# A streaming encoder step: the gate's third of the modulation summed on VectorE instead of TensorE

## The chip, the cores and the metric

The kernel runs on one core of one Trainium2 chip. The metric is the device time of one execution in microseconds (us). A core has TensorE (PE, matrix products), VectorE (DVE), ScalarE (ACT), GpSimd (POOL) and SyncE (SP, which here only issues DMAs), all running their own programs in order and waiting for each other by semaphores.

## What is computed

A one-layer encoder. Each row of x is normalised, scaled and shifted by terms that come from a conditioning vector c, and projected; attention and a pooling mixer run on the projections, and the result is gated by a third term from c. The part that matters here:

```python
def ada_terms(c, w_ada, b_ada):
    m = jax.nn.silu(c) @ w_ada + b_ada          # w_ada is 1024 x 3072
    shift, scale, gate = jnp.split(m, 3, axis=-1)
    return shift, scale, gate

def project(x, c, norm_g, w_ada, b_ada, w_in, b_f):
    shift, scale, gate = ada_terms(c, w_ada, b_ada)
    h = rmsnorm(x, norm_g) * (1.0 + scale[:, None, :]) + shift[:, None, :]
    p = h @ w_in
    ...

def merge(x, attn, ag, pool, pg, gate, w_out):
    z = jnp.concatenate([attn * jax.nn.silu(ag), pool * jax.nn.silu(pg)], axis=-1)
    return x + gate[:, None, :] * (z @ w_out)
```

There are 2048 prompt rows and 64 sample rows, with a c of their own each: two vectors of 1024. Shift and scale are needed before the first projection, the gate only in `merge`, the last stage.

## The kernel before, in words

The kernel has three stages, one behind the other: `stage_project`, attention and the output. The change lies in `stage_project`, which has three phases.

**Start.** SP issues the loads in the order of its program: the first two thirds of w_ada (`slab`), the weights of the value projection (`vraw`), and then the gate's third of w_ada (`graw`, four DMAs of 1 MB). TensorE forms shift and scale with `slab` and the two silu vectors (`pair`, two columns for each of the eight k tiles of 128 rows).

**Value phase.** A loop over 17 tiles of 128 rows. For each, TensorE turns rows (`turn`, into the PSUM pair `xps`), VectorE modulates (`modulate`), ScalarE and GpSimd split the result into a high and a low part (`hhi`, `hlo`), and TensorE multiplies (`value`, L552). Before the tile with `t == GATE_AT` (3) TensorE runs `gate()` (L537): 16 matmuls with a 2-column stationary and 512 moving columns, in fp32, into one slot of `xps`; VectorE adds the bias (L917) and SP stores the row to `scratch_gate`.

**Projection tiles.** 20 tiles of 128 output columns in the order K0, Q0, U0, PG0, and so on (numbered 0 to 19), each of five chunks of columns (three of 512, two of 288; `acc` is a ring of five PSUM banks). Every engine walks the one list `PROJECT_EVENTS` in order and does its own part of each entry. An entry ("weights", n+1) stands at the head of tile n: SP loads the weights of the next tile into `wraw`, ScalarE rounds them to `whi` (L706), GpSimd forms `wlo` (L514). For a chunk of K or Q ScalarE writes `ohi` (L780), VectorE `olo` (L959), the "split", and SP stores both. Entry "f_turn" at the end of tile 0 makes SP issue 22 small DMAs; "k_rows" stores a K chunk in another layout and comes one chunk later. `mps` is a ring of three PSUM banks for these side products. ScalarE writes the chunks of a U tile to `u`, from which VectorE makes the pooling sums.

These lines show how a list entry ties the engines together, on SP and on VectorE:

```python
            for kind, x in PROJECT_EVENTS:
                if kind == "weights":
                    load_weights(sp, x)
                elif kind == "chunk":
                    if x.i >= 1:
                        store_chunk(sp, TILE_CHUNKS[x.i - 1])
...
                if kind == "chunk" and x.tile.split:
                    use = HL_USES[x.i]
                    dve.wait_ge(split_hi, SPLIT_CHUNKS.index(x.i) + 1)
```

## Time and profile before

| | |
|---|---|
| three runs | 1428.19 us median (1426.74 to 1432.84) |
| the profiled execution | 1433.23 us, of which the span of the core 1431.5 us |
| TensorE busy | 1298.6 us (91%), 7007 matmul records |
| VectorE busy | 716.8 us (50%) |
| ScalarE busy | 569.9 us (40%) |
| GpSimd busy | 179.6 us (13%) |
| mean granted TensorE clock | 0.945 of full speed |

The profile is a record of one execution. Times in it are in us from the start of the span. A timeline line gives start, length, engine, source line, operation, output<-input, the count of merged instructions, and in brackets the idle time of the engine before it with what ended that. A line of stretches gives the length, then busy time and count for PE, PE's weight loads, DVE, ACT and POOL, then the granted clock and the DMA share. One fp32 matmul leaves two records.

### The profile page before, as it was taken

To read this page: it belongs to the slowest core of one execution; us is meant where nothing else is said; L and a number is where in the kernel's file an instruction comes from. 1 tells how busy PE (TensorE), PEld (TensorE's weight loads), DVE (VectorE), ACT (ScalarE), POOL (GpSimd) and SP (SyncE) were. 2 spreads that over 40 slices of the span, in tenths; PEclk is the share of its full clock that TensorE was granted. 3 is DMA by queue.
4 is the path that set the end of the run, shared out by engine and by line. 5 is a ranking of instruction groups with operands and counts; after the bars stand their busy time and mean duration, and the time that the engine had idled before them with its cause. 6 is when DMAs were issued, how large, how long until landed. Compare 5 with 4: busy or idle time off the path is not lost. (4 is left out here: it accounts for less than half of the span.)

```text
span 1431.5 us, 19348 instructions
## 1 busy us (share of the span) xinstructions
PE 1298.6 (91%) x7007; PEld 1049.6 (73%) x7007; DVE 716.8 (50%) x1973; ACT 569.9 (40%) x1158; POOL 179.6 (13%) x196
## 2 busy tenths in 40 slices
PE   7899999999999999995699989999999991599996
PEld 1779988888888888885576676767767671488884
DVE  1646433244461111000588877888788881334434
ACT  3546411212112121111477676776777670211111
POOL 1213301101001010100000230131032023000000
PEclk9899999999999999998599999999999995799998
DMA  9636344112213434223913655739456413756662
GB/s 365 232 118 195 141 140 127 60 46 76 87 46 126 155 123 142 88 68 97 199 21 57 105 96 122 136 70 173 82 100 105 94 31 104 251 162 192 206 191 88
DMA packets 159644, 179.51 MB, mean 125 GB/s; under 512 B 34073, under 2 KB 123533, under 8 KB 154878
## 3 DMA queue, kind: packets, MB, share of 16 engines
q1 hardware_dynamic: 153294, 155.21, 42.0%
q10 hardware_dynamic: 5824, 21.50, 4.5%
q8 instruction: 56, 0.92, 0.3%
q0 software_dynamic: 432, 1.57, 0.3%
q14 instruction: 38, 0.31, 0.1%
HBM read 111.55 MB, written 66.69 MB: 125 GB/s over the span
## 5 line engine op out<-in xcount | busy, mean ns | idle before, releaser
L597 PE MATMUL prj_acc<-prj_hhi,til_whi 128*128 128x512 f32 (+1 forms) x800 | 286.5, 358 | 0.0
L599 PE MATMUL prj_acc<-prj_hlo,til_whi 128*128 128x512 f32 (+1 forms) x800 | 284.1, 355 | 0.0
L598 PE MATMUL prj_acc<-prj_hhi,til_wlo 128*128 128x512 f32 (+1 forms) x800 | 284.1, 355 | 0.0
L1386 ACT ACTIVATE att_whi<-att_tps 128x512 fp32r<-128x512 f32 x336 | 169.2, 516 | 118.8 <-PE att_tps L1352 116.0
L1416 DVE TENSOR_TENSOR att_wlo<-att_tps,att_whi 128x512 fp32r<-128x512 f32 x336 | 189.9, 584 | 32.1 <-ACT att_whi L1386 31.8
L1406 DVE TENSOR_SCALAR_CACHE_REDUCE att_wx<-att_sps 128x512 f32<-128x512 f32 x192 | 113.4, 619 | 131.0 <-PE att_sps L1337 127.0
L1336 PE MATMUL att_sps<-att_ka,att_qa 128*128 128x512 f32 (+4 forms) x328 | 153.3, 467 | 25.6 <-DMA att_kb<-scratch_fkd 23.7
L599 PEld LDWEIGHTS prj_acc<-prj_hlo,til_whi 128*128 128x128 f32 x800 | 150.8, 189 | 21.4
L597 PEld LDWEIGHTS prj_acc<-prj_hhi,til_whi 128*128 128x128 f32 x800 | 150.8, 189 | 20.9
L598 PEld LDWEIGHTS prj_acc<-prj_hhi,til_wlo 128*128 128x128 f32 x800 | 150.9, 189 | 20.7
L1524 PE MATMUL fin_acc<-fin_whi,fin_zh 128*128 128x512 f32 (+1 forms) x272 | 106.8, 393 | 45.1 <-DMA fin_zl<-scratch_z 45.1
L1364 PE MATMUL att_ops<-att_whi,att_vt 128*128 128x512 f32 x336 | 140.2, 418 | 0.0
L1352 PE MATMUL att_tps<-keep_ident,att_wx 128*128 128x128 f32 x672 | 118.1, 297 | 12.1 <-ACT att_wx L1380 7.4
L1337 PE MATMUL att_sps<-att_kb,att_qb 68*128 68x512 f32 (+4 forms) x328 | 126.9, 387 | 0.0
L1364 PE MATMUL att_ops<-att_wlo,att_vt 128*128 128x512 f32 x336 | 124.3, 371 | 0.0
L1352 PEld LDWEIGHTS att_tps<-keep_ident,att_wx 128*128 128x128 f32 x672 | 84.5, 151 | 43.9 <-issue 23.4
L1380 ACT ACTIVATE att_wx<-att_wx,att_nm 128x1024 f32<-128x1024 f32 (+1 forms) x96 | 99.0, 1033 | 29.5 <-DVE att_nm L1411 29.5
L1525 PE MATMUL fin_acc<-fin_wlo,fin_zh 128*128 128x512 f32 (+1 forms) x272 | 106.6, 392 | 0.0
L1526 PE MATMUL fin_acc<-fin_whi,fin_zl 128*128 128x512 f32 (+1 forms) x272 | 106.4, 391 | 0.0
L959 DVE SCALAR_TENSOR_TENSOR til_olo<-prj_acc,til_ohi 128x512 fp32r<-128x512 f32 (+1 forms) x40 | 23.8, 597 | 155.0 <-ACT til_ohi L780 155.0
L1336 PEld LDWEIGHTS att_sps<-att_ka,att_qa 128*128 128x128 f32 (+1 forms) x328 | 67.5, 206 | 45.3 <-DMA att_kb<-scratch_fkd 23.9
L514 POOL TENSOR_TENSOR til_wlo<-til_wraw,til_whi 128x1024 fp32r<-128x1024 f32 x20 | 48.1, 2406 | 408.7 <-ACT til_whi L706 408.7
(182 smaller groups left out, 1915.5 us busy)
## 6 DMA issues: line engine op xcount, KB each, us to landing
til_wraw<-in_w_in SPq DMA_DIRECT2D x20, 512.0 KB, 4.2
att_ka<-scratch_k SPq DMA_DIRECT2D x16, 560.0 KB
scratch_v<-val_vs SPq DMA_DIRECT2D x17, 512.0 KB, 4.4
att_qa<-scratch_q SPq DMA_DIRECT2D x16, 528.0 KB
val_xt<-in_x_prompt ACTq DMA_DIRECT2D x16, 512.0 KB, 4.4
ini_al<-in_w_ada SPq DMA_DIRECT2D x8, 1024.0 KB, 15.7
fin_zh<-scratch_z SPq DMA_DIRECT2D x16, 512.0 KB, 4.4
fin_zl<-scratch_z SPq DMA_DIRECT2D x16, 512.0 KB, 5.8
```

What stands on the lines that cost most here:

```text
L597: pe.matmul(out, w[0][:, k, :], hhi[:, k, cs], start=(k == 0), stop=False)
L598: pe.matmul(out, w[1][:, k, :], hhi[:, k, cs], start=False, stop=False)
L599: mm = pe.matmul(out, w[0][:, k, :], hlo[:, k, cs], start=False, stop=(k == KT - 1))
L1336: pe.matmul(bank[0:x.m, 0:x.n], qa[e][:, q], ka[e][:, k], start=True, stop=False)
L1337: mm = pe.matmul(bank[0:x.m, 0:x.n], qb[e][:, q], kb[e][:, k], start=False, stop=not x.last)
L1352: mm = pe.transpose(bank[:, t * P:(t + 1) * P], weights(st, 4 * st.c + t)[:, x.w0:x.w0 + P], keep["ident"][:, :])
L1364: mm = pe.matmul(bank[:, x.skip:x.width], vt[e][0:x.keys, x.tile, :], part[b][0:x.keys, x.skip:x.width], start=(x.first and part is whi), ...
L1386: act.activation(whi[x.i % W_RING][0:x.keys, x.skip:x.width], tps[x.i % T_RING][0:x.keys, x.skip:x.width], ACT.Copy).then_inc(hi_ok, 1)
L1406: dve.tensor_scalar(weights(st, x.row)[0:x.m, x.w0:x.w0 + x.n], sps[x.i % S_RING][0:x.m, 0:x.n], 1.0, None, ALU.mult, ALU.max, accum_out=t ...
L1416: dve.tensor_tensor(wlo[b][0:x.keys, x.skip:x.width], tps[x.i % T_RING][0:x.keys, x.skip:x.width], raw(whi[b][0:x.keys, x.skip:x.width]), ...
L1524: pe.matmul(out, zh[b][:, k, 0:n], whi[:, k, cols], start=(k == 0), stop=False)
L1525: pe.matmul(out, zh[b][:, k, 0:n], wlo[:, k, cols], start=False, stop=False)
```

## The change

The gate's matmuls leave the value phase, and so do the load of the gate's third of w_ada, its bias, the addition and the store. In their place the list gets entries in the tiles 0 and 1:

- "gate_in" x (SP): load the k tile x of the gate's weights, 128 x 1024 fp32 (512 KB), into one of two slots of `gw`. From x = 2 on it waits until both sums of k tile x-2 are done.
- "gate" x (VectorE): for each of the two vectors one pass over 128 x 1024: `gs[w] = gw * pair` (x = 0, `tensor_scalar`) or `gs[w] += gw * pair` (x >= 1, `scalar_tensor_tensor`).
- "gate_bias" (SP): load of the bias into `gw`.
- "gate_sum" 0 and 1, behind the last chunk of tile 1: TensorE adds up the 128 partitions with the constant `pick`, two fp32 matmuls of 512 columns for each half; VectorE adds the bias; SP stores to `scratch_gate`.

`gw` and `gs` share memory with `u`, so the first chunk of tile 2 waits on ScalarE for the store of the gate. The waits on `g_ok` and `g_out` in the value phase go, and `turn` uses the two `xps` slots in plain alternation.

```diff
@@ project_events
+    gates = {(0, 3): [("gate_in", 0), ("gate_in", 1)], (0, 4): [("gate", 0), ("gate_in", 2)],
+             (1, 0): [("gate", 1), ("gate_in", 3), ("gate", 2), ("gate_in", 4)],
+             (1, 1): [("gate", 3), ("gate_in", 5), ("gate", 4), ("gate_in", 6)],
+             (1, 2): [("gate", 5), ("gate_in", 7), ("gate", 6)], (1, 3): [("gate", 7), ("gate_bias", 0)],
+             (1, 4): [("gate_sum", 0), ("gate_sum", 1)]}
...
+            ev += gates.get((t.n, c), [])
@@ SP
-            for k in range(0, KT, 2):
-                sp.dma_start(graw[:, k:k + 2, :], wada[:, k:k + 2, 2 * D:]).then_inc(g_in, 16)
-            sp.wait_ge(m_full, 1)
-            sp.dma_start(gate_b, io["b_ada"][:, 2 * D:].partition_broadcast(2)).then_inc(gb_in, 16)
...
-                if t == GATE_AT:
-                    sp.wait_ge(g_ok, 2)
-                    sp.dma_start(dram["gate"][:, :], grow).then_inc(g_out, 16)
...
+                elif kind == "gate_in":
+                    if x >= 2:
+                        sp.wait_ge(ga_ok, 2 * (x - 1))
+                    sp.dma_start(gw[:, x % 2, :], wada[:, x, 2 * D:]).then_inc(g_in[x % 2], 16)
+                elif kind == "gate_bias":
+                    sp.wait_ge(ga_ok, 2 * (KT - 1))
+                    sp.dma_start(gate_b, io["b_ada"][:, 2 * D:].partition_broadcast(2)).then_inc(gb_in, 16)
+                elif kind == "gate_sum" and x == 1:
+                    m_wait(sp, m_free, ("gate_sum", 1), 1)
+                    sp.dma_start(dram["gate"][:, :], grow).then_inc(g_out, 16)
@@ TensorE
-                if t == GATE_AT:
-                    gate()
...
+                elif kind == "gate_sum":
+                    pe.wait_ge(pick_ok, 3)
+                    pe.wait_ge(ga_ok, 2 * KT)
+                    for w in range(2):
+                        mm = pe.matmul(bank[0:2, :], pick[:, 2 * w:2 * w + 2], gs[:, w, x * 512:(x + 1) * 512],
+                                       start=(w == 0), stop=(w == 1))
+                    mm.then_inc(m_done, 1)
@@ ScalarE
-                if t == KT:
-                    act.wait_ge(g_out, 16)
...
+                        if x.c == 0 and t.g == 0:
+                            act.wait_ge(g_out, 16)
@@ VectorE
-                if t == GATE_AT:
-                    dve.wait_ge(g_full, 1)
-                    dve.wait_ge(gb_in, 16)
-                    for n in range(2):
-                        cs = slice(n * 512, (n + 1) * 512)
-                        dve.tensor_tensor(grow[:, cs], xps[GATE_SLOT][0:2, cs], gate_b[:, cs], ALU.add).then_inc(g_ok, 1)
...
+                elif kind == "gate":
+                    dve.wait_ge(g_in[x % 2], 16 * (x // 2 + 1))
+                    for w in range(2):
+                        if x == 0:
+                            ins = dve.tensor_scalar(gs[:, w, :], gw[:, 0, :], pair[:, 0, w:w + 1], None, ALU.mult)
+                        else:
+                            dve.wait_ge(ga_ok, 2 * x - 1 + w)
+                            ins = dve.scalar_tensor_tensor(out=gs[:, w, :], in0=gw[:, x % 2, :], scalar=pair[:, x, w:w + 1],
+                                                           in1=gs[:, w, :], op0=ALU.mult, op1=ALU.add)
+                        ins.then_inc(ga_ok, 1)
+                elif kind == "gate_sum":
+                    m_wait(dve, m_done, ("gate_sum", x), 1)
+                    dve.wait_ge(gb_in, 16)
+                    cs = slice(x * 512, (x + 1) * 512)
+                    dve.tensor_tensor(grow[:, cs], mps[M_USES["gate_sum", x].slot][0:2, :], gate_b[:, cs], ALU.add).then_inc(m_free, 1)
```

On VectorE the row of instructions from the first chunk of tile 1 on was, before:

```order
L959 SCALAR_TENSOR_TENSOR til_olo<-prj_acc,til_ohi 128x512 [waits prj_t_split_hi]
L992 COPY til_row<-prj_mps 128x128 [waits prj_row_out0,prj_t_m_done]
L992 COPY til_row<-prj_mps 96x128
L992 COPY til_row<-prj_mps 64x128
L959 SCALAR_TENSOR_TENSOR til_olo<-prj_acc,til_ohi 128x512 [waits prj_t_split_hi] x2
```

and is now, in the same place (`prj_g_in0` and `prj_g_in1` are the landings in the two slots of `gw`):

```order
L955 SCALAR_TENSOR_TENSOR til_olo<-prj_acc,til_ohi 128x512 [waits prj_t_split_hi]
L1003 COPY til_row<-prj_mps 128x128 [waits prj_row_out0,prj_t_m_done]
L1003 COPY til_row<-prj_mps 96x128
L1003 COPY til_row<-prj_mps 64x128
L986 SCALAR_TENSOR_TENSOR gat_gs<-gat_gw,prj_silu,gat_gs 128x1024 [waits prj_ga_ok,prj_g_in1]
L986 SCALAR_TENSOR_TENSOR gat_gs<-gat_gw,prj_silu,gat_gs 128x1024 [waits prj_ga_ok]
L986 SCALAR_TENSOR_TENSOR gat_gs<-gat_gw,prj_silu,gat_gs 128x1024 [waits prj_ga_ok,prj_g_in0]
L986 SCALAR_TENSOR_TENSOR gat_gs<-gat_gw,prj_silu,gat_gs 128x1024 [waits prj_ga_ok]
L955 SCALAR_TENSOR_TENSOR til_olo<-prj_acc,til_ohi 128x512 [waits prj_t_split_hi]
```

The sums of k tiles 1 and 2 stand behind the split of the first chunk and its k_rows copies; those of 3 and 4, 5 and 6, and 7 follow behind the splits of the next three chunks.

On SP the same stretch, before:

```order
L465 DMA out_k_prompt<-til_row 128x2x128 [waits prj_t_m_free]
L465 DMA out_k_prompt<-til_row 32x128
L377 DMA til_wraw<-in_w_in 128x8x128 [waits prj_t_wt_lo]
L386 DMA scratch_k<-til_ohi 128x288 [waits prj_t_free_d]
L387 DMA scratch_k<-til_olo 128x288
L465 DMA out_k_prompt<-til_row 128x128 [waits prj_t_m_free]
L465 DMA out_k_prompt<-til_row 96x128
L465 DMA out_k_sample<-til_row 64x128
L386 DMA scratch_q<-til_ohi 128x512 [waits prj_t_free_d]
L387 DMA scratch_q<-til_olo 128x512
```

and now:

```order
L459 DMA gat_gw<-in_w_ada 128x1024 [waits prj_ga_ok]
L380 DMA til_wraw<-in_w_in 128x8x128 [waits prj_t_wt_lo]
L389 DMA scratch_k<-til_ohi 128x288 [waits prj_t_free_d]
L390 DMA scratch_k<-til_olo 128x288
L471 DMA out_k_prompt<-til_row 128x128 [waits prj_t_m_free]
L471 DMA out_k_prompt<-til_row 96x128
L471 DMA out_k_sample<-til_row 64x128
L459 DMA gat_gw<-in_w_ada 128x1024 [waits prj_ga_ok] x2
L389 DMA scratch_q<-til_ohi 128x512 [waits prj_t_free_d]
L390 DMA scratch_q<-til_olo 128x512
L459 DMA gat_gw<-in_w_ada 128x1024 [waits prj_ga_ok] x2
```

The first of these rows is the load of k tile 2, ahead of the weights of tile 2; the two pairs are those of the k tiles 3 and 4, and 5 and 6, each waiting for sums of VectorE; the load of k tile 7 follows behind the next pair of Q stores. The two loads without a wait (k tiles 0 and 1) stand in tile 0, ahead of the 22 DMAs of "f_turn".

## Rows read from the trace of the kernel before

**Rows 1.** Stretches of the project stage; columns as told above, clock before DMA share.
```profile
49.00:71.00 22.00, 21.97 (x161) 21.54 (x162) 11.06 (x43) 11.47 (x21) 7.18 (x3) 0.88 0.50 163
71.00:85.30 14.30, 14.30 (x41) 3.41 (x39) 3.19 (x11) 4.00 (x7) 2.35 (x1) 1.00 0.31 99
85.30:176.00 90.70, 90.70 (x765) 90.45 (x763) 49.98 (x186) 49.75 (x91) 30.04 (x13) 1.00 0.51 161
176.00:250.00 74.00, 72.24 (x373) 61.64 (x373) 27.34 (x71) 15.29 (x30) 7.20 (x3) 0.98 0.45 133
```

**Rows 2.** Timeline of TensorE around the gate's matmuls.
```profile
70.61 13.89 PE L537 MATMUL vps_xps<-ini_ah,prj_silu 128*2 128x512 f32 x32
84.44 0.77 PE L529 MATMUL vps_xps<-keep_ident,val_xn 128*128 128x128 f32 x5
```

**Rows 3.** Timeline of TensorE, the turns of two successive tiles of the value phase.
```profile
91.13 1.04 PE L529 MATMUL vps_xps<-keep_ident,val_xn 128*128 128x128 f32 x8
...
97.77 1.04 PE L529 MATMUL vps_xps<-keep_ident,val_xn 128*128 128x128 f32 x8
```

**Rows 4.** Timeline of TensorE, the first matmul of tile 2.
```profile
229.85 0.39 PE L597 MATMUL prj_acc<-prj_hhi,til_whi 128*128 128x512 f32 x1
```

**Rows 5.** Timeline of SP: k_rows in tile 0, end of f_turn, weights of tile 2.
```profile
204.29 0.39 SPq L465 DMA_DIRECT2D out_k_prompt<-til_row  x1
...
216.35 0.30 SPq L459 DMA_DIRECT2D scratch_fkd<-fgt_fr  x1
...
217.65 0.42 SPq L377 DMA_DIRECT2D til_wraw<-in_w_in  x1
```

**Rows 6.** Timeline of ScalarE: weights of tile 2, then tile 1's first two chunks.
```profile
222.12 1.06 ACT L706 ACTIVATE til_whi<-til_wraw 128x1024 fp32r<-128x1024 f32 x1 [15.05 <-DMA til_wraw<-in_w_in]
223.09 1.07 ACT L780 ACTIVATE til_ohi<-prj_acc 128x512 fp32r<-128x512 f32 x2
```

**Rows 7.** Timeline of VectorE: end of tile 0, split of tile 1's first chunk, k_rows.
```profile
208.25 0.60 DVE L992 COPY til_row<-prj_mps 128x256 f32<-128x256 f32 x2
223.70 0.69 DVE L959 SCALAR_TENSOR_TENSOR til_olo<-prj_acc,til_ohi 128x512 fp32r<-128x512 f32 x1 [14.85 <-ACT til_ohi L780]
224.31 0.67 DVE L992 COPY til_row<-prj_mps 128x128 f32<-128x128 f32 x3
```

**Rows 8.** Line 1574, a scalar_tensor_tensor on VectorE: durations in ns min/median/max.
```profile
L1574 DVE SCALAR_TENSOR_TENSOR fin_o<-fin_y,fin_st,fin_fg x17: 1277/1285/1286, 1259.2 to 1426.8; 128x1024 f32<-128x1024 f32 x16, 64x1024 f32<-64x1024 f32 x1
```

**Rows 9.** Line 655, loads of x, 512 KB each: issue, and issue to landing.
```profile
L655 ACTq DMA_DIRECT2D val_xt<-in_x_prompt x16: 334/335/446, 0.8 to 133.4; - x16
...
DMA to landing us min/median/max: 3.6/4.4/8.6
```

**Rows 10.** Line 377, loads of projection weights, 512 KB each, likewise.
```profile
L377 SPq DMA_DIRECT2D til_wraw<-in_w_in x20: 380/433/1226, 166.7 to 616.5; - x20
...
DMA to landing us min/median/max: 3.9/4.2/5.3
```

**Rows 11.** Stretches behind idle time of TensorE: one in tile 0, two in attention.
```profile
184.00:190.00 6.00, 6.00 (x21) 4.83 (x21) 2.42 (x12) 2.52 (x4) 2.39 (x1) 0.72 0.17 50
...
690.00:695.00 5.00, 5.00 (x13) 3.60 (x13) 4.12 (x12) 1.36 (x3) 0.00 (x0) 0.50 1.17 208
...
705.00:710.00 5.00, 5.00 (x21) 3.88 (x20) 2.38 (x8) 2.03 (x5) 0.00 (x0) 0.53 1.00 211
```

**Rows 12.** Longest wait of TensorE in front of attention: us in total, times, longest.
```profile
PE att_sps L1336 <- DMA att_kb<-scratch_fkd: 23.7, 1, 23.7
```

**Rows 13.** Timeline, two VectorE operations of one shape, the second beside a GpSimd one.
```profile
273.98 0.69 DVE L1019 TENSOR_TENSOR til_olo<-til_row,til_ohi 128x512 fp32r<-128x512 f32 x1 [0.70 <-ACT til_ohi L797]
...
284.55 2.41 POOL L514 TENSOR_TENSOR til_wlo<-til_wraw,til_whi 128x1024 fp32r<-128x1024 f32 x1 [27.50 <-ACT til_whi L706]
...
286.11 1.39 DVE L1019 TENSOR_TENSOR til_olo<-til_row,til_ohi 128x512 fp32r<-128x512 f32 x1 [0.70 <-ACT til_ohi L797]
```

**Rows 14.** Timeline of ScalarE: weights of tile 3.
```profile
238.73 1.06 ACT L706 ACTIVATE til_whi<-til_wraw 128x1024 fp32r<-128x1024 f32 x1 [4.72 <-DMA til_wraw<-in_w_in]
```

More of the change, by code:

```diff
@@ L144, in chunk_in @@
     return lambda kind, x: kind == "chunk" and x.tile.kind in kinds
-M_USES = uses(lambda kind, x: kind in ("cache", "state", "f_sum", "f_turn", "k_rows", "mix", "tails"), M_RING)
+M_USES = uses(lambda kind, x: kind in ("cache", "state", "f_sum", "f_turn", "k_rows", "mix", "tails", "gate_sum"), M_RING)
 F_EV = {}
@@ L200, in stage_project @@
         tri = s.sb("tri", [P, P])
+        pick = s.sb("pick", [P, 4])
         with Scope(nc, "val") as a:
@@ L230, in stage_project @@
             gsc = b.sb("gsc", [P, T])
+            with Scope(nc, "gat") as g:
+                gw = g.sb("gw", [P, 2, D])
+                gs = g.sb("gs", [P, 2, D])
+            u = b.sb("u", [P, U_ALL])
+            dhi = [b.sb(f"dhi{n}", [P, 512], F32R) for n in range(D_RING)]
+            dlo = [b.sb(f"dlo{n}", [P, 512], F32R) for n in range(D_RING)]
             sa = b.sb("sa", [P, HIST + 512])
             sb_ = b.sb("sb", [P, HIST + 512])
-            dhi = [b.sb(f"dhi{n}", [P, 512], F32R) for n in range(D_RING)]
-            dlo = [b.sb(f"dlo{n}", [P, 512], F32R) for n in range(D_RING)]
         with Scope(nc, "vps") as a:
@@ L252, in stage_project @@
         x_in = [s.sem(f"x_in{n}") for n in range(2)]
+        g_in = [s.sem(f"g_in{n}") for n in range(2)]
         v_out = [s.sem(f"v_out{n}") for n in range(2)]
@@ L530, in turn @@
                 mm.then_inc(xturn, 1)
-            def gate():
-                pe.wait_ge(g_in, 64)
-                pe.wait_ge(hf_ok, KT * (GATE_AT + 1))
-                for n in range(2):
-                    for k in range(KT):
-                        mm = pe.matmul(xps[GATE_SLOT][0:2, n * 512:(n + 1) * 512], pair[:, k, :], graw[:, k, n * 512:(n + 1) * 512],
-                                       start=(k == 0), stop=(k == KT - 1))
-                mm.then_inc(g_full, 1)
             def value(t):
@@ L770, in _ @@
                     elif t.kind == "U":
-                        if x.c == 0 and t.g >= 1:
+                        if x.c == 0 and t.g == 0:
+                            act.wait_ge(g_out, 16)
+                        elif x.c == 0:
                             act.wait_ge(d_ok, NP * t.g)
@@ L911, in _ @@
             for t in range(NT):
-                if t == GATE_AT:
-                    dve.wait_ge(g_full, 1)
-                    dve.wait_ge(gb_in, 16)
-                    for n in range(2):
-                        cs = slice(n * 512, (n + 1) * 512)
-                        dve.tensor_tensor(grow[:, cs], xps[GATE_SLOT][0:2, cs], gate_b[:, cs], ALU.add).then_inc(g_ok, 1)
                 if t + 4 < NT:
```

31 lines of the change are left out of this document (12 added, 19 removed).

## The prediction

> **What bounds the kernel now.** I read the stretches of the project stage first [rows 1]. TensorE is busy in 21.97 of 22.00 us before the gate's matmuls, in all 14.30 around them, in all 90.70 behind them and in 72.24 of 74.00 in the first projection tiles. So in this stage whatever TensorE executes or waits for is paid in full, and VectorE, busy 27.34 of 74.00 us in the last stretch, has room on average. The question is not room but the order in which VectorE, ScalarE and SP come to their instructions, so the second view is the timelines of these three around the end of tile 0 and in tile 1.
>
> **What is removed: 13.8 us of TensorE.** The gate's 16 matmuls (32 records) begin at 70.61, and the next turn begins at 84.44 [rows 2]: 13.83 us, or 0.865 us for one matmul at full clock. Nothing covers it. The other engines could have used this pause to get ahead, so is it really saved? Successive turns of the value phase come 6.64 us apart (91.13 and 97.77) with TensorE without a gap [rows 3], the stretch before the pause was as full as the one behind it [rows 1], and each engine is tied to TensorE's products tile by tile; the others keep up without the pause. I count all 13.8. The 4 MB of gate weights also leave the start, where I count nothing: TensorE's own matmuls fill the time until shift and scale are there, and the turn, modulation and split behind them wait for no load. VectorE's addition (within the pause) and the store go with it.
>
> **What is added on TensorE: 3.5 us and a wait.** The four matmuls of "gate_sum" have the moving size and type of the removed ones: 4 x 0.865 = 3.5 us at full clock. They stand in front of tile 2 and need the last of the sixteen passes of VectorE. I work out when that is in the times of the trace of before (all of it lies 13.8 us earlier in the changed kernel, which changes no difference). TensorE gets to the place at 229.85 [rows 4].
>
> **When VectorE can begin.** Its copies of tile 0 end about 208.8 [rows 7]. The loads of the k tiles 0 and 1 are issued behind the k_rows store of 204.29 [rows 5] and land before 210, and "gate" 0 runs then; two passes of at most 1.29 us each, in an idle stretch of 14.85 us [rows 7], cost nothing. "gate" 1, though, stands behind the split of tile 1's first chunk. Before, that split ran only at 223.70, since ScalarE had first to round the weights of tile 2 (222.12, [rows 6]), which SP had issued at 217.65, behind the row of small DMAs that ends at 216.35 [rows 5]. The k_rows copies follow until 224.9 [rows 7]. This cascade did not hurt before, because `acc` has five banks; now it sets the start of the sums. The change makes it later: SP issues two gate loads ahead of these DMAs and one directly ahead of the weights, 3 x 0.43 = 1.3 us [rows 10], and the weights' data come behind 512 KB more. The trace has no such pair here; it costs between nothing and a whole load of 4.2 us [rows 10], and I take 0.5, near the low end, since the DMA engines are busy 0.45 of the time in this stretch [rows 1]. "gate" 1 begins at 224.9 + 1.8 = 226.7.
>
> **How long the sums take.** A pass is a scalar_tensor_tensor over 128 x 1024; line 1574 has one of this size at 1.285 us [rows 8], so a k tile costs 2.6 us. The first pass starts while GpSimd forms `wlo` of tile 2. Two tensor_tensors of one shape on VectorE took 0.69 us alone and 1.39 us beside GpSimd's 2.41 us operation [rows 13]; I add 0.7 once. "gate" 1 ends at 226.7 + 2.6 + 0.7 = 230.0, when TensorE has just arrived with six k tiles still to come. `gw` has two slots: the load of k tile 3 is issued when "gate" 1 ends, that of 5 when 3 ends, that of 7 when 5 ends. Each round is a load plus two passes. A 512 KB load with the same 4 KB rows lands 4.4 us after its issue (3.6 at least, [rows 9]); the weights' loads of this size took 3.9 to 5.3 [rows 10]. So 3 x (4.4 + 2.6) = 21.0, and the sums end at 251.0. The even k tiles and the splits fit into the gaps. Behind the waits on SP the stores of Q are queued, and so ScalarE's `ohi` of the later chunks; nobody on TensorE needs those before tile 3. The wait of TensorE is 251.0 - 229.85 = 21.1 us.
>
> **The clock.** After idle time TensorE runs at half clock (1.2 GHz) for a while. Behind a short idle of some 2 us in tile 0 the stretch of 6.00 us has a clock of 0.72: a loss of 6.00 x 0.28 = 1.7 us [rows 11]. I take 2.0, as it is the row with the same matmuls behind the wait.
>
> **What is late next.** The gate's store lies ahead of the weights of tile 3 on SP, and ScalarE's first chunk of tile 2 waits for it. Before, these weights came at 238.73 [rows 14], 8.9 us after tile 2 began and some 14 us before tile 3 did. In the changed kernel the additions, the store and the load put them at 7 to 9 us behind the start of tile 2, the same cover. I count nothing.
>
> **The sum.** -13.8 + 21.1 + 3.5 + 2.0 = +12.8 us. The profiled execution took 1433.2, so its like would be 1446.0; on the median of 1428.2 it is 1441.0. The change is slower by 0.9%.
>
> **Bounds.** Least: no queueing, issues of 0.33 [rows 9], no collision with GpSimd, loads of 3.6: the first sum ends at 228.5, the last at 228.5 + 3 x 6.2 = 247.1, a wait of 17.2, in all -13.8 + 17.2 + 3.5 + 1.7 = +8.6. Most: the weights 4.2 us later for the queue, loads of 5.3: 224.9 + 5.5 + 2.6 + 0.7 = 233.7, then 3 x 7.9, a wait of 27.5 and +19.2.
>
> **Rivals.** (1) The loads do not bind, and the sums run back to back: from 230.0 six times 2.6 and three splits (0.69, 0.69, 0.46) to 247.5, a wait of 17.6, +9.3 us, 1437.5. For it speaks only the 3.6 us minimum; against it the order on SP, which issues a load when its slot is free. The Trainium skill, "DMA: Bandwidth & Descriptors" (Anatomy of one DMA), gives a transfer about 2.0 us plus its bytes at 436 GB/s, an estimate of 3.2 us for these 512 KB against the 4.4 of the trace; by that page the loads just cease to bind and this rival's time comes out. The page's figure is for another issuing path than SP's, so I follow the rows. Chance 0.12, a quarter of which falls within 0.5%.
>
> (2) The clock stays low. In attention, behind an idle of 23.7 us [rows 12], as long as the one forecast here, the clock is 0.50 to 0.53 in stretches from 690 to 710 although TensorE is busy in both of the stretches shown [rows 11]: 20 us at half speed, a loss of 10 instead of 2.0, in all +20.8, 1449.0. Against it: there DMAs saturate and the products have other shapes, while here the same fp32r matmuls follow as in tile 0. The Trainium skill, "TensorE: Matmul & The Clock Gate" (Why this matters for your kernels), says that an idle gap between bursts puts the engine back to half clock and that keeping it busy regains full clock. By it the loss is the small one and the sum 12.8; the rows of attention show a busy engine that stayed low, and by them it is 20.8. Chance 0.10.
>
> (3) Faster: the sums are done before TensorE comes. The place is "gate" 1 on VectorE, which has its data since about 210 and an idle engine; if it and the rest were not held behind the split, only 3.5 us of matmuls stay, -13.8 + 3.5 = -10.3 us, 1417.9. It decides by the wait: under 13.8 - 3.5 - 2.0 = 8.3 us the change wins. For that the last sum would have to end by 238, and between 224.9 and there not even the seven k tiles fit (18 us). Against it stands the order in program and list, which no timing changes. Chance 0.07. (4) Something in between, VectorE free several us earlier, a wait of 8 to 15 us: 0.07, within 0.5%.
>
> **How the numbers follow.** The forecast, a wait of 17 to 25 us and a short ramp, has 0.64. Faster by over 0.5% (about 7 us, what a measurement of this kernel can tell from no change): 0.07. Within 0.5%: 0.07 + 0.03 = 0.10. Slower: 0.64 + 0.09 + 0.10 = 0.83. The range 1434 to 1450 takes in rivals 1 and 2, both bounds and the scatter of the runs before; out of it are rivals 3 and 4 and some tails.
>
> **What would show it.** Right: TensorE has no L537 group, turns 6.64 us apart from the first tile on, and one new idle of about 21 us before the "gate_sum" matmuls, released by VectorE's `gat_gs`; VectorE's `gat_gs` passes last 1.28 us each, with idle before those of k tiles 3, 5 and 7 that ends by a DMA into `gat_gw`; the clock of the stretch is under 1. The weights of tile 2 land 1 to 3 us later relative to TensorE. Wrong: a wait under 8 us, a stretch of the value phase in which TensorE waits for `hlo`, or a new wait in front of tile 3 or a mix.

## The result, and the profile after

The changed kernel takes 1447.05 us (median of 4 runs, 1443.85 to 1448.21) against 1430.51 us for the kernel before (4 runs, 1426.74 to 1434.45). The ratio is 1.0118, with a 95% interval of 1.0097 to 1.0140: slower by 1.2%, some 16.5 us. The forecast was slower by 12.8 us. The two profiled executions took 1446.8 and 1433.2 us and differ by 13.6 us, in their times as in their spans (1445.1 and 1431.5). The interval of the ratio is 13.9 to 20.0 us; 14.7 us of the loss can be followed in the traces, up to the end of the project stage.

The longest waits of TensorE after the change (us in total, times, longest). The first two are old ones of other stages (the kernel before has 45.1 us in the place of the first, and the second is that of [rows 12]); the third is new.

```profile
PE fin_acc L1535 <- DMA fin_zl<-scratch_z: 45.9, 1, 45.9
PE att_sps L1347 <- DMA att_kb<-scratch_fkd: 24.1, 1, 24.1
PE prj_mps L631 <- DVE gat_gs L986: 22.0, 1, 22.0
```

Timeline of TensorE: two turns of the value phase in the place where the gate's matmuls stood [rows 2, 3], then the end of tile 1, the gate's additions, and the start of tile 2 [rows 4].

```profile
63.47 1.03 PE L535 MATMUL vps_xps<-keep_ident,val_xn 128*128 128x128 f32 x8
...
70.12 1.03 PE L535 MATMUL vps_xps<-keep_ident,val_xn 128*128 128x128 f32 x8
...
215.49 0.29 PE L594 MATMUL prj_acc<-prj_hlo,til_whi 128*128 128x288 f32 x1
237.75 5.50 PE L631 MATMUL prj_mps<-gat_gs,prj_pick 128*2 128x512 f32 x8 [21.97 <-DVE gat_gs L986]
243.19 0.50 PE L592 MATMUL prj_acc<-prj_hhi,til_whi 128*128 128x512 f32 x1
```

The pause of 13.83 us is gone: the turns follow each other in 6.65 us. (One trace could be luck, so I looked at all of them: the first projection tile begins at 161.3 to 162.7 us in the nine traces of kernels without the pause and at 175.3 to 176.3 in the five with it. The means are 13.7 us apart, and the start of this stage is good to some 1 us in a single trace.) TensorE comes to the additions at 237.75 - 21.97 = 215.78, which is 229.85 - 14.07. There it waits 21.97 us and spends 5.44 us until tile 2 begins: -14.07 + 21.97 + 5.44 = +13.34, and 229.85 + 13.34 is the 243.19 of the last row. The rest of this section says what the 21.97 are made of.

Timeline of VectorE in the changed kernel (L955 is the split, L1003 the k_rows copies, L983 the two passes of the first k tile, L986 the other fourteen), to be compared with [rows 7]:

```profile
195.16 1.42 DVE L983 TENSOR_SCALAR gat_gs<-gat_gw,prj_silu 128x1024 f32<-128x1024 f32 x2 [0.58 <-DMA gat_gw<-in_w_ada]
213.79 0.69 DVE L955 SCALAR_TENSOR_TENSOR til_olo<-prj_acc,til_ohi 128x512 fp32r<-128x512 f32 x1 [17.21 <-ACT til_ohi L782]
214.40 0.67 DVE L1003 COPY til_row<-prj_mps 128x128 f32<-128x128 f32 x3
214.99 5.44 DVE L986 SCALAR_TENSOR_TENSOR gat_gs<-gat_gw,prj_silu,gat_gs 128x1024 f32<-128x1024 f32 x4
220.34 0.69 DVE L955 SCALAR_TENSOR_TENSOR til_olo<-prj_acc,til_ohi 128x512 fp32r<-128x512 f32 x1
221.74 2.48 DVE L986 SCALAR_TENSOR_TENSOR gat_gs<-gat_gw,prj_silu,gat_gs 128x1024 f32<-128x1024 f32 x2 [0.71 <-DMA gat_gw<-in_w_ada]
225.17 2.48 DVE L986 SCALAR_TENSOR_TENSOR gat_gs<-gat_gw,prj_silu,gat_gs 128x1024 f32<-128x1024 f32 x2 [0.95 <-DMA gat_gw<-in_w_ada]
...
231.75 2.48 DVE L986 SCALAR_TENSOR_TENSOR gat_gs<-gat_gw,prj_silu,gat_gs 128x1024 f32<-128x1024 f32 x2 [1.11 <-DMA gat_gw<-in_w_ada]
...
235.13 2.48 DVE L986 SCALAR_TENSOR_TENSOR gat_gs<-gat_gw,prj_silu,gat_gs 128x1024 f32<-128x1024 f32 x2 [0.53 <-DMA gat_gw<-in_w_ada]
```

This is the sequence of the prediction: the first k tile at once in the idle stretch (two operations, 1.42 us), then 17.21 us of nothing, because the second k tile stands behind the split and the split behind ScalarE. When TensorE arrives (215.78) VectorE is in the first of the fourteen passes. From there on the idle pieces in front of the passes end by a load into `gat_gw`: those of the k tiles 3, 4, 6 and 7.

Timeline of SP (L459 are the gate's loads, L443 to L455 the small DMAs of "f_turn", L380 the weights) and, last, ScalarE's rounding of the weights of tile 2, to be compared with [rows 5, 6]:

```profile
190.41 1.00 SPq L459 DMA_DIRECT2D gat_gw<-in_w_ada  x2
...
192.72 0.80 SPq L443 DMA_DIRECT2D out_logf_prompt<-prj_lf  x1
193.57 3.44 SPq L444 DMA_DIRECT2D out_logf_sample<-prj_lf  x1
197.12 1.47 SPq L451 DMA_DIRECT2D scratch_fqp<-fgt_fhi  x1
...
205.25 0.29 SPq L455 DMA_DIRECT2D scratch_fkd<-fgt_fr  x1
...
206.55 0.42 SPq L459 DMA_DIRECT2D gat_gw<-in_w_ada  x1
207.01 0.43 SPq L380 DMA_DIRECT2D til_wraw<-in_w_in  x1
```

```profile
212.22 1.06 ACT L706 ACTIVATE til_whi<-til_wraw 128x1024 fp32r<-128x1024 f32 x1 [19.42 <-DMA til_wraw<-in_w_in]
```

Taken back by the 14.07 us, the weights of tile 2 were issued at 203.58 and rounded from 208.05 on in the kernel before. Now it is 207.01 (+3.4) and 212.22 (+4.2). The forecast had 1.8 for this.

Durations of the passes (ns, min/median/max) and the landing of the eight gate loads (us), against [rows 8, 9]:

```profile
L986 DVE SCALAR_TENSOR_TENSOR gat_gs<-gat_gw,prj_silu,gat_gs x14: 1274/1280/1841, 215.0 to 236.3; 128x1024 f32<-128x1024 f32 x14
```

```profile
DMA to landing us min/median/max: 3.6/4.2/5.4
```

The pass of 1841 ns is the first, the one that ran beside GpSimd's operation of 2.40 us. It took 0.56 us more than the others:

```profile
213.35 2.40 POOL L524 TENSOR_TENSOR til_wlo<-til_wraw,til_whi 128x1024 fp32r<-128x1024 f32 x1 [39.47 <-ACT til_whi L706]
```

The clock behind the wait is the last view here, in the columns of [rows 1] (the 0.64 and the 1.00 are the granted clock):

```profile
238.00:243.00 5.00, 5.00 (x8) 0.68 (x6) 0.68 (x1) 0.00 (x0) 0.00 (x0) 0.64 0.00 0
243.00:247.00 4.00, 4.00 (x17) 3.11 (x17) 1.70 (x3) 0.00 (x0) 0.00 (x0) 1.00 0.32 50
```

TensorE is back at full clock when tile 2 starts.

### The profile page after: what moved, and what is told of

Same layout as the page of the kernel before. It is cut to its first block and busy times, and to the rows that moved or that the text cites. A ratio compares the mean times of both kernels' runs of the same rounds, so it can differ in the third digit from the quotient of the medians.

```text
span 1445.1 us, 19332 instructions
## 1 busy us (share of the span) xinstructions
PE 1289.1 (89%) x6983; PEld 1043.9 (72%) x6983; DVE 734.7 (51%) x1989; ACT 569.1 (39%) x1158; POOL 179.7 (12%) x199
## 5 line engine op out<-in xcount | busy, mean ns | idle before, releaser
L592 PEld LDWEIGHTS prj_acc<-prj_hhi,til_whi 128*128 128x128 f32 x800 | 151.0, 189 | 22.6 <-issue 0.9
L1363 PE MATMUL att_tps<-keep_ident,att_wx 128*128 128x128 f32 x672 | 118.3, 297 | 12.8 <-ACT att_wx L1391 8.2
L524 POOL TENSOR_TENSOR til_wlo<-til_wraw,til_whi 128x1024 fp32r<-128x1024 f32 x20 | 48.1, 2404 | 437.5 <-ACT til_whi L706 437.5
L955 DVE SCALAR_TENSOR_TENSOR til_olo<-prj_acc,til_ohi 128x512 fp32r<-128x512 f32 (+1 forms) x40 | 23.8, 597 | 150.6 <-ACT til_ohi L782 150.6
```

Of the source, the lines that this page charges most:

```text
L592: pe.matmul(out, w[0][:, k, :], hhi[:, k, cs], start=(k == 0), stop=False)
L1363: mm = pe.transpose(bank[:, t * P:(t + 1) * P], weights(st, 4 * st.c + t)[:, x.w0:x.w0 + P], keep["ident"][:, :])
```

## Where the 22 us come from: the passes left out, the loads left out

First I took the suspected cause away in two ways.

**No passes.** Loads and passes of the k tiles 1 to 7 are left out, so the gate is formed from one k tile; nothing else changes.

```diff
-    gates = {(0, 3): [("gate_in", 0), ("gate_in", 1)], (0, 4): [("gate", 0), ("gate_in", 2)],
-             (1, 0): [("gate", 1), ...
+    gates = {(0, 3): [("gate_in", 0)], (0, 4): [("gate", 0)], (1, 3): [("gate_bias", 0)],
...
-                    pe.wait_ge(ga_ok, 2 * KT)
+                    pe.wait_ge(ga_ok, 2)
```

> The loads and passes of the k tiles 1 to 7 are left out; gate_sum stays behind tile 1 and adds up k tile 0 alone (so the gate is not the reference's). My theory: the value phase saves its 13.8 to 14.1 us in full and the loss lies in the wait for the passes alone, so TensorE has no idle in front of gate_sum, pays 3.5 us of matmuls at full clock, and the time is before -10.5 us, about 1420. Rival (the pause in the value phase let other engines get ahead, or the move costs something elsewhere, as a new wait in front of tile 3 or a mix): some of the 14 us comes back, 1424 or more.

Measured: 1424.93 us (10 runs), ratio to the kernel before 0.9951, interval 0.9933 to 0.9968. No wait in front of the additions is left in the trace, and the span is 1419.3 us, 25.8 under that of the changed kernel. So the loss comes with the loads and passes of these k tiles, which end too late; the next kernel parts the two. Without them the move gains: by the times 7 to 8 us (4.6 to 9.6 by the interval), by the end of the project stage 10.6 us. Of these 10.6, 1.5 are no part of it: in this execution the short fall of the clock in tile 0 [rows 11] did not occur, and tile 0 took 29.2 us instead of 30.7. The 9.1 that remain stand against the 10.3 of the prediction (the 13.8 us of the pause less the 3.5 us of additions), and a later section finds the missing 1.2.

**No loads.** Now the passes stay, but the loads of the k tiles 2 to 7 are left out (each pass reads what its slot holds, so the gate is not the true one). If loads bind the sums, this must shorten them; if only VectorE does, nothing changes.

```diff
-             (1, 0): [("gate", 1), ("gate_in", 3), ("gate", 2), ("gate_in", 4)],
+             (1, 0): [("gate", 1), ("gate", 2)],
...
-                    dve.wait_ge(g_in[x % 2], 16 * (x // 2 + 1))
+                    dve.wait_ge(g_in[x % 2], 16)
```

> The changed kernel with the loads of the k tiles 2 to 7 left out: the passes read what the two slots hold (the gate is not the reference's). My theory (behind the first two k tiles each round waits for a load): the seven k tiles and three splits run back to back, about 19.5 us from the start of gate 1, against 22.6 in the changed kernel, and the start is about 1 us earlier; TensorE waits about 18 us instead of 22.0. Rival (the loads cost nothing beside the passes): 21 to 22 us as before.

Measured: 1438.66 us (one run), span 1436.9. The wait, and VectorE's timeline without a gap (the rows of k tiles 1 to 7 and the splits between them):

```profile
PE prj_mps L631 <- DVE gat_gs L986: 17.3, 1, 17.3
```

```profile
212.83 5.45 DVE L986 SCALAR_TENSOR_TENSOR gat_gs<-gat_gw,prj_silu,gat_gs 128x1024 f32<-128x1024 f32 x4
218.19 0.69 DVE L955 SCALAR_TENSOR_TENSOR til_olo<-prj_acc,til_ohi 128x512 fp32r<-128x512 f32 x1
218.79 4.87 DVE L986 SCALAR_TENSOR_TENSOR gat_gs<-gat_gw,prj_silu,gat_gs 128x1024 f32<-128x1024 f32 x4
223.57 0.69 DVE L955 SCALAR_TENSOR_TENSOR til_olo<-prj_acc,til_ohi 128x512 fp32r<-128x512 f32 x1
224.18 4.87 DVE L986 SCALAR_TENSOR_TENSOR gat_gs<-gat_gw,prj_silu,gat_gs 128x1024 f32<-128x1024 f32 x4
228.96 0.46 DVE L955 SCALAR_TENSOR_TENSOR til_olo<-prj_acc,til_ohi 128x288 fp32r<-128x288 f32 x1
229.32 2.48 DVE L986 SCALAR_TENSOR_TENSOR gat_gs<-gat_gw,prj_silu,gat_gs 128x1024 f32<-128x1024 f32 x2
```

The sums take 212.83 to 231.8 = 19.0 us here, 214.99 to 237.6 = 22.6 with the loads. So the loads cost 3.6 us by binding the sums, and 1.0 by delaying their start relative to TensorE; 17.3 of the 22.0 us stay even with data that is always there. The wait is above all one of VectorE, which starts too late; the two slots of `gw` are second. One detail: four passes take 4.87 us, and the next row begins 4.78 after them, so two passes cost 2.4 us in a row and not twice 1.28. In the trace successive passes overlap by some 0.08 us.

## Three repairs

**Weights first.** SP issues the weights of tile 2 in tile 0, ahead of the gate's loads (and not again at their old place), so that ScalarE and the split no longer wait for them.

```diff
                 elif kind == "gate_in":
+                    if x == 0:
+                        load_weights(sp, 2)
```

> One change to the changed kernel: SP issues the weights of tile 2 in tile 0, ahead of the first gate load and of the 22 small DMAs. My theory (the sums start late because VectorE stands behind a split that waits for ScalarE, which waits for these weights): the first chunk of tile 1 is split at about 199 instead of 213.8, gate 1 starts there, the other loads follow behind the small DMAs, the last sum ends about 230 instead of 237.6, TensorE waits 14 to 15 us instead of 22.0, and the time is 7 to 8 us under the changed kernel, about 1439. Rival (the 22 us are the time of the sums themselves on VectorE, wherever they start): wait and time as in the changed kernel, 1446 to 1447.

**The sum later.** The additions stand behind the third chunk of tile 2 instead of in front of that tile, so that TensorE has work until they are ready.

```diff
-             (1, 4): [("gate_sum", 0), ("gate_sum", 1)]}
...
+            if (t.n, c) == (2, 2):
+                ev += [("gate_sum", 0), ("gate_sum", 1)]
```

> One change to the changed kernel: gate_sum stands behind the third chunk of tile 2 instead of the last of tile 1. My theory (the loss is nothing but TensorE's wait in order): the sums end at the same place, TensorE does three chunks (16.7 us) meanwhile, waits about 1.3 us for the bank of the third chunk, whose split is late, and about 4 us in front of gate_sum; before -4 to -5 us, about 1426. Rival (ScalarE, held by the gate's store, gives the banks back late, or the pooling sums come late for the mixes): new waits in tile 3 and 4 eat 5 us and more, 1431 or above.

**Both.**

> The changes of the last two kernels together. My theory: the sums end about 230, before TensorE comes to gate_sum at about 232.5, no wait is left, only the matmuls of gate_sum at full clock: before -10.5 us, about 1420, the same as without the passes. Rival (late banks or late pooling sums): a wait of TensorE behind tile 2, 1424 or more.

| kernel | time us (runs) | ratio to before, 95% | wait for `gat_gs` | project stage ends |
|---|---|---|---|---|
| before | 1433.27 (25) | | | 665.1 |
| changed | 1447.05 (4) | 1.0118, 1.0097 to 1.0140 | 22.0 | 679.8 |
| weights first | 1446.1 (4) | 1.0101, 1.0073 to 1.0129 | 15.0 | 674.4 |
| sum later | 1433.16 (10) | 1.0006, 0.9988 to 1.0025 | 3.3 | 663.5 |
| both | 1427.27 (10) | 0.9965, 0.9944 to 0.9986 | none | 657.3 |

The last column is the end of the last projection matmul in the trace. The time of the changed kernel is from its own comparison, the others were measured together on one chip, so the ratios are to be compared and not the times. In the trace the first repair takes 7.0 us off the wait and 5.4 us off the stage (its first projection tile began 1.2 us later, and the additions took 0.3 more). The times alone don't show it (0.17% less, with intervals that overlap). The second takes off 16.3 us, and this the times do show.

The waits came as expected in all three, but the gains in time did not. Expected were 7 to 8 us less than the changed kernel, then 4 to 5 and 10.5 us less than the kernel before. The ratios say 2.4 less than the changed kernel, then 0.9 more and 5.0 less than the kernel before (each good to some 3 or 4 us). The placement effect below takes 1.2 us from the last two, and in these traces the first projection tile began 1.0 to 1.4 us later than in the changed kernel. The rest, some 3 to 4 us in each, is not explained. One hint: TensorE's wait in front of the output stage is 47.4 to 48.1 us in the traces of these three kernels and of the one without passes, all taken on one chip, and 43.9 to 46.0 in all others, so a difference of spans between one of these four traces and another has 2 us in it that no edit made.

VectorE's row in the first repair says why the wait does not fall further. "gate" 1 now begins at 202.03, but the load of k tile 2 still stands behind the row of small DMAs, and VectorE idles for it:

```profile
213.03 2.48 DVE L989 SCALAR_TENSOR_TENSOR gat_gs<-gat_gw,prj_silu,gat_gs 128x1024 f32<-128x1024 f32 x2 [8.54 <-DMA gat_gw<-in_w_ada]
```

With the sum later, TensorE waits at two places instead of one: 3.3 us for the sums, and 1.2 us ahead of them for a bank of `acc` that VectorE's split frees late, since the splits are behind passes.

```profile
PE prj_mps L632 <- DVE gat_gs L987: 3.3, 1, 3.3
...
PE prj_acc L593 <- DVE til_olo L956: 1.2, 1, 1.2
```

With both, the additions stand in TensorE's row without idle time ahead of them and take 3.5 us at full clock, a term of the prediction that the changed kernel itself could not show:

```profile
L635 PE MATMUL prj_mps<-gat_gs,prj_pick x8: 592/593/593, 234.0 to 237.0; 128*2 128x512 f32 x8
```

## Why VectorE starts 4.2 us late and not 1.8

The move of the weights has two parts in the trace: SP issues them 3.4 us later, of which the three gate loads ahead explain 1.4 (1.00 and 0.42), and they land 0.7 us later after that. The missing 2.0 us are in the row of small DMAs for the forget sums. Its members at lines 443, 444 and 451 take 0.80, 3.44 and 1.47 us to issue, where the kernel before had 0.44, 2.79 and 0.52. Is that the 1 MB of gate loads in flight, or only the moment? In the next kernel SP issues the gate loads 0 and 1 behind this row instead of ahead of it, and load 2 behind the weights of tile 2.

```diff
-    gates = {(0, 3): [("gate_in", 0), ("gate_in", 1)], (0, 4): [("gate", 0), ("gate_in", 2)],
-             (1, 0): [("gate", 1), ("gate_in", 3), ...
+    gates = {(0, 4): [("gate_in", 0), ("gate_in", 1), ("gate", 0)],
+             (1, 0): [("gate_in", 2), ("gate", 1), ("gate_in", 3), ...
```

> The changed kernel with the gate's loads 0 and 1 moved on SP behind the row of small DMAs for the forget sums in tile 0, and load 2 moved to tile 1. It asks why the sums began 4.2 us later than in the kernel before where 1.8 was forecast. Theory C (the small DMAs take longer to issue because 1 MB of gate loads is in flight: 3.44 and 1.47 us for the two groups, 2.79 and 0.52 before): here they take 2.8 to 3.0 and 0.5 to 0.7 us again. Theory D (the difference is the moment at which they come, beside the weights and stores of the last value tiles, since the changed kernel gets there 14 us earlier): they stay at 3.3 to 3.5 and 1.4 to 1.7. In both the first load of the sums is late itself, so the wait is 20 to 24 us; the time is 1440 to 1450.

Measured: 1444.51 us (one run), wait 21.0. Timeline of SP in this kernel:

```profile
193.05 0.39 SPq L443 DMA_DIRECT2D out_logf_prompt<-prj_lf  x1
193.49 1.01 SPq L444 DMA_DIRECT2D out_logf_sample<-prj_lf  x1
195.31 0.33 SPq L451 DMA_DIRECT2D scratch_fqp<-fgt_fhi  x1
...
202.33 0.29 SPq L455 DMA_DIRECT2D scratch_fkd<-fgt_fr  x1
...
203.63 0.90 SPq L459 DMA_DIRECT2D gat_gw<-in_w_ada  x2
204.57 0.43 SPq L380 DMA_DIRECT2D til_wraw<-in_w_in  x1
```

The row takes 9.6 us (193.05 to 202.62) against 12.8 in the changed kernel and 10.9 in the kernel before, at nearly the same moment of the program. So it is not the moment: theory D falls. Theory C holds for the row, and the other traces bear it out. The row takes 12.5 to 12.9 us in the four with two 512 KB loads issued just ahead, 13.0 to 13.8 in the three with three of them (the weights too), 11.1 in the one with one, and 9.2 to 11.2 in the six with none. It does not hold for line 444 alone, which fell below what it forecast: without any such load ahead it took 1.0 to 1.2 us in four traces and 2.8 and 3.1 in two, both of the unchanged kernel before; in three of the four the store just ahead of the row took 1.5 to 2.0 us instead of 0.45. Something else can hold SP up too, and what it is stays open. The DMA issue of SP is in any case not a fixed 0.43 us. The weights are back at the place that they had before (11.0 us behind ScalarE's `fhi` here and before, 14.6 in the changed kernel), and the sums start 2.8 us earlier relative to TensorE's work. But the wait falls by only 1.0 us, because the load of k tile 2 now comes late (VectorE is idle 2.38 us for it):

```profile
218.76 2.48 DVE L986 SCALAR_TENSOR_TENSOR gat_gs<-gat_gw,prj_silu,gat_gs 128x1024 f32<-128x1024 f32 x2 [2.38 <-DMA gat_gw<-in_w_ada]
```

What the one order gains, the other nearly loses; only the weights ahead of everything, as in the repair above, took more off the wait (7.0 us).

## The last 1.4 us: what a small tile does to its neighbours

From the start of tile 2 to the end of the project stage the changed kernel takes 1.4 us longer than the kernel before (436.6 against 435.2), with no wait in it. The projection matmuls simply follow each other more slowly. My suspicion is that it is where their tiles lie: `pick`, 16 bytes per partition, is new among the tiles in front of them. So I put unused tiles of 16, 64 and 128 bytes per partition into the kernel before, and widened `pick` to 64. For a sense of what is noise, the kernel before also ran once more unchanged. The edit with 16 bytes (4 fp32 elements):

```diff
         tri = s.sb("tri", [P, P])
+        pad = s.sb("pad", [P, 4])
```

The recorded texts follow; the last of them was written together with the first two, ahead of the other three.

> The kernel before once more, unchanged, as a yardstick for the comparison itself. Both theories: ratio 1.000 within 0.2%. It also gives a second trace of it: if 512-column projection matmuls follow each other in 232.4 ns in this trace too (against 233.5 in the changed kernel and all its variants), that difference is one of the programs and not of the execution; and it shows how much the attention stage (542.8 us in the first trace, 541.5 to 547.2 in the variants) varies from one execution to the next.

> The kernel before with one unused tile of 16 bytes per partition in the place where the changed kernel has pick. Theory A (the projection tiles of the changed kernel and its variants are 1.6 us longer in sum because pick moves the weights tiles by 16 bytes): spacing of the 512-column matmuls 233.5 ns, project stage 1.6 us longer, time +1.6 us. Theory B (the spacing comes from something else, as the longer program or the gate's traffic): spacing 232.4, time as before.

> The kernel before with one unused tile of 64 bytes per partition where the changed kernel has its 16-byte tile of ones; nothing else is different. In the run of the version with both repairs and a 64-byte tile the spacing of the 512-column projection matmuls was 229.2 ns, against 232.4 in the kernel before, 233.4 with 16 bytes. Theory A (the placement alone does it, whatever the gate does): spacing 229.2 here too, the project stage (first projection tile to its end, 489.4 us before) 4 to 7 us shorter, the time 0.3 to 0.5% under the kernel before, 1422 to 1426. Theory B (the shorter spacing came with the order of the changed kernel, where the gate's tiles also moved the tiles behind them): spacing 232 to 233.5, project stage 489 to 491, the time within 0.15% of the kernel before.

> The kernel before with one unused tile of 128 bytes per partition in the place of the 64-byte one; nothing else is different. Spacing of the 512-column projection matmuls so far by what lies ahead of the weight tiles: 232.4 ns with nothing, 233.4 with 16 bytes, 229.7 with 64. Theory P (the placement counts in steps that repeat every 128 bytes, so that 128 more is the same as nothing): spacing 232.4, project stage 489 to 490 us, the time within 0.15% of the kernel before. Theory Q (any odd or even number of 64 bytes is alike, nothing having been the exception, or the rule is a longer one): spacing 229.2 to 231.5 or above 233, project stage 2 to 6 us shorter or 1 to 2 us longer, the time under the kernel before by 0.1 to 0.5% or over it by 0.1%.

> The changed kernel as it is, with 64 bytes per partition instead of 16 for the tile of ones; the wait of 22 us before the additions stays. Theory A (placement acts by itself and adds to the rest): wait 21.5 to 22.5 us, spacing 229.2 ns instead of 233.5, project stage about 7 us shorter than in the changed kernel (518.4 there), time 1438 to 1441, a ratio of 1.005 to 1.008 to the kernel before. Theory B (the gain of the version with both repairs was mostly a faster attention stage in the executions drawn): project stage within 2 us of 518, ratio 1.010 to 1.013.

> The last kernel (weights of tile 2 first, gate_sum behind the third chunk of tile 2) with pick enlarged from 16 to 64 bytes per partition and nothing else. Theory A: spacing back to 232.4 ns, 1.6 us under that kernel's project stage, about before -7 to -9 us. Theory B: no change against it, about -5 to -6 us.

Lines of the first of the three products of the projection, the group that [rows 4] belongs to (durations in ns min/median/max, then first and last start in us): the kernel before, then with 16, 64 and 128 bytes in front.

```profile
L597 PE MATMUL prj_acc<-prj_hhi,til_whi x800: 288/392/795, 175.6 to 664.5; 128*128 128x512 f32 x100, 128*128 128x288 f32 x60
```

```profile
L598 PE MATMUL prj_acc<-prj_hhi,til_whi x800: 292/392/796, 175.3 to 665.4; 128*128 128x512 f32 x100, 128*128 128x288 f32 x60
```

```profile
L598 PE MATMUL prj_acc<-prj_hhi,til_whi x800: 289/388/505, 175.9 to 659.4; 128*128 128x512 f32 x100, 128*128 128x288 f32 x60
```

```profile
L598 PE MATMUL prj_acc<-prj_hhi,til_whi x800: 292/389/747, 176.3 to 657.5; 128*128 128x512 f32 x100, 128*128 128x288 f32 x60
```

First to last start: 488.9, 490.1, 483.5, 481.2 us (in the third execution the clock did not fall in tile 0, which is worth 1.7 us). The table has the mean distance of successive 512-column matmuls, and the stretch from the start of tile 3 to the end of the stage, where no wait differs:

| kernel | bytes in front | distance ns | tile 3 to end us | time us (runs) | ratio to before, 95% |
|---|---|---|---|---|---|
| before, again | 0 | 232.4 | 412.1 | 1431.57 (10) | 1.0017, 0.9999 to 1.0035 |
| before | 16 | 233.4 | 413.2 | 1431.68 (10) | 1.0012, 0.9993 to 1.0032 |
| before | 64 | 229.7 | 409.0 | 1424.32 (10) | 0.9956, 0.9941 to 0.9971 |
| before | 128 | 227.2 | 405.4 | 1426.87 (10) | 0.9969, 0.9954 to 0.9984 |
| changed | 16 | 233.5 | 413.3 | 1447.05 (4) | 1.0118, 1.0097 to 1.0140 |
| changed | 64 | 229.2 | 408.3 | 1437.54 (4) | 1.0065, 1.0043 to 1.0088 |
| both repairs | 16 | 233.5 | 413.3 | 1427.27 (10) | 0.9965, 0.9944 to 0.9986 |
| both repairs | 64 | 229.2 | 408.3 | 1418.52 (4) | 0.9911, 0.9884 to 0.9938 |

The 16 bytes alone give the 1.1 to 1.2 us in the trace (413.2 and 413.3 against 412.1), which the times can't resolve. With 64 bytes the stretch is 3.1 us shorter than with none and 4.2 to 5.0 shorter than with 16, in all three kernels, and the time is 0.4 to 0.5% (6 to 8 us) shorter. The stretch alone is not all of that; where the rest arises is not shown. Two of the recorded expectations missed: the version with both repairs and 64 bytes was to come back to 232.4 ns and came to 229.2, and TensorE's wait in the changed kernel with 64 bytes was 22.9 us where 21.5 to 22.5 was expected. In the version with both repairs and 64 bytes TensorE waits 0.9 us for the sums, where it waited for nothing with 16.

128 bytes give still more in the stretch, so the steps don't repeat after 128 bytes (theory P falls). The time does not follow: 0.9969 against 0.9956, with intervals that overlap, where the stretch alone would give 3.6 us more. In the two traces the spans are 1422.4 us with 128 bytes and 1423.6 with 64, so no stage is seen that lost it, and this stays open. Which tile's address counts, and by what rule, stays open too: a tile in front moves all behind it.

This has a consequence for every comparison here. Measured at one placement, the change costs 1.0118 / 1.0012 = 1.011 with 16 bytes and 1.0065 / 0.9956 = 1.011 with 64; both repairs bring 0.9965 / 1.0012 = 0.995 and 0.9911 / 0.9956 = 0.995, each good to some 0.3% by the intervals. The best kernel, both repairs with 64 bytes, is 0.9% faster than the kernel before, and only half of that is the gate's.

## The prediction, point by point

The forecast was +12.8 us, and +16.5 was measured. The chain behind it was the right one: a pause saved, a wait for VectorE paid in its place. The wait (21.1 us forecast, 22.0 measured) came out close partly by luck, since two terms of it were off in opposite directions, as told below.

**The removal, 13.8 us: right.** 14.07 us at the end of tile 1, 13.7 in the mean of all traces, and the turns run through without a gap. **The additions and the clock, 3.5 + 2.0: right.** 5.44 us in the changed kernel, 3.5 us where nothing is waited for. Rival 2, a clock that stays low, is excluded at this place: 0.64 until 243.0, 1.00 from there. The Trainium skill, "TensorE: Matmul & The Clock Gate" (Why this matters for your kernels), lets a busy engine regain full clock, and the trace agrees here (1.00 from 243.0 on). In attention the clock was 0.50 to 0.53 in the two stretches of [rows 11]. But they were not a clean case against the rule: between them TensorE was busy only 2.98 of 5.00 us, which the prediction did not see.

```profile
700.00:705.00 5.00, 2.98 (x11) 2.32 (x11) 2.53 (x10) 3.97 (x7) 0.00 (x0) 0.50 1.02 218
```

**The start of "gate" 1: 1.8 forecast, 4.2 measured.** The cascade (loads ahead on SP, weights later, ScalarE, split, passes) was the right one. The term was too small because I took SP's issue as a constant: 1.3 us for three loads. The row of small DMAs behind them grew by 1.9 us, and the kernel with the loads behind the row shows that the loads do it. The queue's 0.5 was about right (0.7).

**The collision with GpSimd: 0.7 forecast, 0.56 measured.**

**The rounds: 21.0 forecast, 19.6 measured**, from the end of "gate" 1 at 218.0 to 237.6. SP issues the loads of the k tiles 3, 5 and 7 at 218.06, 224.25 and 230.67 (the first of each row):

```profile
218.06 2.73 SPq L459 DMA_DIRECT2D gat_gw<-in_w_ada  x2
...
224.25 3.76 SPq L459 DMA_DIRECT2D gat_gw<-in_w_ada  x2
...
230.67 0.33 SPq L459 DMA_DIRECT2D gat_gw<-in_w_ada  x1
```

The rounds are 6.2, 6.4 and 7.0 us: 2.5 us of passes, not 2.6, and some 4.0 from the issue to their start, not 4.4. The forecast had the idle time in front of the k tiles 3, 5 and 7. It is there for 3 and 7 (0.71 and 0.53 us). For k tile 5 there is none: its data had landed while VectorE was at the passes of k tile 4 and the split. The longer idle times, 0.95 and 1.11 us, stand in front of 4 and 6, which the forecast let "fit into the gaps". So the length of the three rounds came out near the forecast for a chain that was only in part the one described. On the wait the errors largely cancel, which is luck: 21.1 + 2.4 - 0.1 - 1.4 = 22.0.

**Rival 1, the loads don't bind: false, and well priced.** VectorE waits for loads in five places (3.9 us in all, the first one of no weight). The prediction put 3.5 us between loads that bind and loads that don't; the sums without loads are 3.6 us shorter (19.0 against 22.6), and another 1.0 us of the wait goes because the weights come earlier. The Trainium skill, "DMA: Bandwidth & Descriptors" (Anatomy of one DMA), gives an estimate of 3.2 us for 512 KB, for DMAs issued by GpSimd. The fastest of the gate's loads, issued by SP, took 3.6 and the median 4.2, and for them the measurement decides.

**Rival 3, faster: false as the change stands; its condition is borne out at both ends and not in between.** "It decides by the wait: under 8.3 us the change wins." With 15.0 us of wait the kernel was slower, with 3.3 + 1.2 about level, with none faster. By the bound, 4.5 us of wait would leave 8.3 - 4.5 = 3.8 of gain; the placement of the next paragraph takes 1.2 of it, the project stage ends 1.6 us before that of the kernel before, and the interval of the ratio (0.9988 to 1.0025) allows 1.7 at most. That a wait between 4.5 and 8.3 us still wins is not shown.

**Missing: the 1.4 us of placement.** No step of the prediction had it, and nothing in the rows of before could have shown it. **What is late next: nothing, as forecast.** ScalarE rounds the weights of tile 3 at 248.71, 5.5 us behind the start of tile 2 (8.9 before, [rows 14]; 7 to 9 forecast), and TensorE does not wait in front of tile 3.

**The rest of the difference.** At the end of the project stage the changed kernel is 14.7 us behind, at the end of the span 13.6, in the medians 16.5. These three numbers differ by less than the later stages vary by from one execution to the next. These are the stretch from 688 to 800 us, the first of attention, in the kernel before and in its repetition (columns of [rows 1]):

```profile
688.00:800.00 112.00, 102.88 (x542) 79.23 (x543) 88.17 (x265) 76.66 (x160) 5.10 (x4) 0.87 0.54 98
```

```profile
688.00:800.00 112.00, 103.47 (x578) 78.43 (x579) 91.24 (x276) 80.53 (x169) 5.10 (x4) 0.95 0.53 100
```

One program, 0.87 against 0.95 of the clock, and 543 against 536 us for attention as a whole (from its first matmul to the first of the output stage). The difference of the spans of two traces is therefore no better than some 7 us. The terms above were taken stage by stage for that reason.

## What to carry to other kernels

Work that is moved onto a half-idle engine costs by the moment at which that engine comes to it, not by its share of idle time: here VectorE had 17 us free directly before the passes and stood behind a wait of its own, and TensorE paid 22 us for 14. Before such a move, follow the chain that releases the receiving engine and every queue that the new loads pass, put the consumer as late as the program allows, and reckon with small DMAs that are issued more slowly behind large ones (the row of 22 took 12.5 to 12.9 us instead of 9.2 to 11.2). And when a new tile is added, however small, compare with a kernel that has the same tile unused, or a placement effect is booked as one of the change.

## What the runs showed of the chip that I had not expected

- The distance of the same 512-column matmuls depends on where their tiles lie: 227.2, 229.2 to 229.7, 232.4 and 233.5 ns, with 128, 64, 0 and 16 bytes per partition in front. From the best to the worst that is 8 us in the stretch from tile 3 on alone, half of what the studied change cost.
- SP's issue of the same row of 22 small DMAs took 9.2 to 11.2 us with no 512 KB load issued just ahead, 11.1 with one, 12.5 to 12.9 with two and 13.0 to 13.8 with three. One DMA of the row took anything from 1.0 to 4.7 us, and 1.0 to 3.1 without a load ahead.
- Two executions of one program had attention stages of 536 and 543 us, with granted clocks of 0.95 and 0.87 in its first 112 us, with TensorE busy 92% of that stretch in both.
